# Attention scores in two parts: the low part of q against the high part of k as two 64-row matmuls in two halves of the array

## The reference

```
s = einsum('bqkgd,bskd->bkgqs', q, k) * HEAD_DIM ** -0.5      # 8 query heads, 2 key heads, HEAD_DIM = 64
p = softmax(s, axis=-1)                                       # over 256 context + 1024 latent keys
o = einsum('bkgqs,bskd->bqkgd', p, v)
```

## Time and profile before

| | |
|---|---|
| median of 3 runs | 2757.2 us (2756.16 to 2759.43) |
| profiled execution: its own time | 2757.11 us |
| its span in the trace | 2755.3 us |
| mean granted TensorE clock | 0.991 |
| TensorE busy (PE), weight loads (PEld) | 97%, 80% of the span |
| VectorE, ScalarE, GpSimd busy | 58%, 31%, 37% |
| scores (L900) on the chain that ended last | 6% |

### The profile page before, as it was taken

The page is one execution under the profiler, slowest core; times in us unless marked ns, Lnnn a source line. Parts: engine busy times, 40 slices in busy tenths (PEclk is TensorE's granted clock), DMA queues, the critical chain, the costliest instruction groups (busy, mean ns, idle before and its releaser), DMA issues.

```text
span 2755.3 us, 32885 instructions
## 1 busy us (share of the span) xinstructions
PE 2672.7 (97%) x13578; PEld 2196.3 (80%) x13578; DVE 1585.6 (58%) x1512; ACT 841.1 (31%) x1220; POOL 1021.2 (37%) x915
## 2 busy tenths in 40 slices
PE   7999999999999999999999899999999999999996
PEld 4888888888887888888878688888888888877874
DVE  3745544541018888847657763555552299866756
ACT  3234444442100000034314423545552000005313
POOL 3721111112224333334575662111114355554573
PEclk9999999999999999999999999999999999999998
DMA  6111111111255111124333512101112211114433
GB/s 264 35 60 35 39 35 39 35 41 62 76 188 212 44 38 39 39 90 149 133 128 126 173 41 69 43 35 35 39 43 81 77 46 47 46 58 145 142 124 113
DMA packets 75892, 224.74 MB, mean 82 GB/s; under 512 B 8672, under 2 KB 12000, under 8 KB 74720
## 3 DMA queue, kind: packets, MB, share of 16 engines
q1 hardware_dynamic: 53280, 182.26, 19.3%
q10 hardware_dynamic: 22464, 40.38, 3.9%
HBM read 177.52 MB, written 45.09 MB: 81 GB/s over the span
## 4 chain that ended last, share of the span: by engine, by line
PE 88%; DVE 6%; ACT 3%; issue 2%; DMA 1%; POOL 0%; SPq 0%; ACTq 0%; DVEq 0%; POOLq 0%
PE PS L733 48%; PE PS L864 20%; PE PS L900 6%; PE PS L922 5%; PE PS L909 5%; PE PS L932 1%; ACT Pr L1205 1%; DVE cv L1683 1%; PE PS L776 1%; DVE e L1756 1%; DMA wmA<-wmod 1%; ACT PTh L1228 1%; PE PS L782 1%; PE PS L886 0%; DMA wraw<-w 0%
## 5 line engine op out<-in xcount | busy, mean ns | idle before, releaser
L622 POOL CAST wh<-wraw 128x512 fp32r<-128x512 f32 (+1 forms) x424 | 333.7, 787 | 1262.8 <-PE PS L733 630.6
L624 POOL TENSOR_TENSOR wl<-wraw,wh 128x512 fp32r<-128x512 f32 (+1 forms) x424 | 611.2, 1441 | 34.0
L1650 DVE TENSOR_TENSOR PTl<-PS,PTh 128x512 fp32r<-128x512 f32 x328 | 226.9, 692 | 417.6 <-ACT PTh L1228 417.5
L733 PE MATMUL PS<-Uh,wh 128*128 128x512 f32 (+1 forms) x1536 | 428.8, 377 | 15.3 <-issue 9.6
L1683 DVE SCALAR_TENSOR_TENSOR cv<-hc,vec,cv 128x1024 f32<-128x1024 f32 x360 | 435.8, 1238 | 8.8
L733 PE MATMUL PS<-Uh,wl 128*128 128x512 f32 (+1 forms) x1536 | 420.4, 371 | 0.0
L733 PE MATMUL PS<-Ul,wh 128*128 128x512 f32 (+1 forms) x1536 | 418.7, 370 | 0.0
L864 PE MATMUL PS<-Uh,wh 128*128 128x512 f32 (+1 forms) x960 | 358.7, 374 | 2.8 <-POOL wl L624 2.3
L864 PE MATMUL PS<-Uh,wl 128*128 128x512 f32 (+1 forms) x960 | 357.1, 372 | 0.0
L864 PE MATMUL PS<-Ul,wh 128*128 128x512 f32 (+1 forms) x960 | 356.9, 372 | 0.0
L1228 ACT ACTIVATE PTh<-PS 128x512 fp32r<-128x512 f32 x328 | 196.2, 598 | 438.8 <-PE PS L909 434.2
(11 more groups left out here) (159 smaller groups left out, 3446.3 us busy)
## 6 DMA issues: line engine op xcount, KB each, us to landing
wraw<-w SPq DMA_DIRECT2D x164, 512.0 KB, 3.4
graw<-stg ACTq DMA_DIRECT2D x88, 256.0 KB, 2.0
wmB<-wmod SPq DMA_DIRECT2D x32, 512.0 KB, 5.7
e<-graw SPq DMA_DIRECT2D x24, 640.0 KB, 3.9
wraw<-w SPq DMA_DIRECT2D x48, 256.0 KB, 4.1
e<-graw SPq DMA_DIRECT2D x24, 512.0 KB, 3.6
wmA<-wmod SPq DMA_DIRECT2D x8, 1024.0 KB, 12.3
hL<-hT_in SPq DMA_DIRECT2D x8, 640.0 KB, 21.1
```

The lines of the kernel that those rows point to most:

```text
L622: nc.gpsimd.tensor_copy(wh[par][:, s], wraw[par][:, s]).then_inc(whi[par], 1)
L624: nc.gpsimd.tensor_tensor(wl[par][:, s], wraw[par][:, s], wh[par][:, s].bitcast(F32), ALU.subtract).then_inc(wsplit[par], 1)
L733: ins = mmul(PS[:, at + c:at + c + m], w[par][:, k * P:(k + 1) * P], x[:, k, c0 + c:c0 + c + m], start=(first and a == 0), stop=(last and ...
L1650: tt(PTl[b][:], PS[:, PT0[bank]:PT0[bank] + 512], PTh[b][:].bitcast(F32), ALU.subtract).then_inc(pt_free[bank], 1)
```

## The change

For a latent unit the three chunks are first multiplied with the high part of q. The low part of q is multiplied with the last chunk (keys 1024 to 1279) as before, with all 128 rows. For keys 0 to 511 and 512 to 1023 it is multiplied with 64 rows only: rows 0 to 63 of the stationary and the moving operand for the first, rows 64 to 127 for the second, into two PSUM banks. So that rows 64 to 127 hold the high part of k there, `k_lo` writes the low part of keys 512 to 1023 to rows 0 to 63. The product low by low, which the matmuls with all rows gave along, is left out for keys 0 to 1023. Context units do what they did.

```diff
@@ scores(un, h)
+                    hi, lo = (x[un % 2][:, h * P:(h + 1) * P] for x in (qTh, qTl))
                     for c, m in chunks(nk * P):
-                        for a, x in enumerate((qTh, qTl)):
-                            ins = mmul(PS[:, s0 + c:s0 + c + m], x[un % 2][:, h * P:(h + 1) * P],
-                                       kT[:, g, k0 * P + c:k0 * P + c + m], start=(a == 0), stop=(a == 1))
+                        mmul(PS[:, s0 + c:s0 + c + m], hi, kT[:, g, k0 * P + c:k0 * P + c + m], start=True, stop=False)
+                    ins = mmul(PS[:, s0 + c:s0 + c + m], lo, kT[:, g, k0 * P + c:k0 * P + c + m], start=False, stop=True)
+                    if nk > 2:
+                        for a in range(2):
+                            rows = slice(a * HD, (a + 1) * HD)
+                            ins = mmul(PS[:, s0 + a * 512:s0 + (a + 1) * 512], lo[rows], kT[rows, g, a * 512:(a + 1) * 512],
+                                       start=False, stop=True)
                     ins.then_inc(s_s, 1)
@@ k_lo(g)
                         dve.wait_ge(s_khi, 6 * l + 3 * g + i + 1)
-                        tt(kT[HD:P, g, c:c + n], tbank(f, n)[HD:P], kT[HD:P, g, c:c + n].bitcast(F32),
+                        rows = slice(0, HD) if i == 1 else slice(HD, P)
+                        tt(kT[rows, g, c:c + n], tbank(f, n)[rows], kT[rows, g, c:c + n].bitcast(F32),
                            ALU.subtract).then_inc(t_free[f % 2], 1)
```

## The result

The changed kernel took 2774.06 us (median of 5 runs, 2771.3 to 2774.68) against 2757.26 of the kernel before: 16.8 us slower (quotient of the medians 1.0061), ratio over all runs 1.0057 with a 95% interval of 1.0042 to 1.0071. A second series (5 runs against 15 of the kernel before) gave 1.0076 (1.0062 to 1.0089), 20.8 us. Forecast was + 20.

A forecast was written before the change was run, and what follows sets the result against it. TensorE was taken to set the pace, busy 97% of the span. Per head + 0.41 - 0.23 = + 0.18 us, times 128 + 23, less 3 absorbed: 2757 + 20 = 2777 us, range 2728 to 2797.

The forecast's parts named there:

- Counts and order: Attention scores: 128 score sums, each keeping six matmuls and six weight loads; the new order costs nothing.
- What is saved: 0.23 us a head: Low-part score matmuls: two halves side by side take one matmul's 0.23 us, saving at most 29 us over 128 sums.
- In 0.19, out 0.22, 0.41 together: TensorE around each 64-row pair: entering costs 0.19 us and leaving 0.22, together 0.41 us per head.
- The choice of 0 for the second half's load: Pair's weight loads: the second half's load adds 0 us; 0.11 more if it waits for the first.
- the one number taken over from another shape: Price of a trip into tiles and back, 0.33 us, read at L797's column tiles and applied to row halves.
- The 0.43 us that the prediction calls a full float32 matmul: At L782, 512 columns take 0.43 us start to start; L797's four tiles take the same, hence fully side by side.
- the loss before absorption: Each head's scores: 0.41 us trip less 0.23 saved gives + 0.18 us, times 128 + 23 us.
- The type costs nothing, the tiles' shape does: Around L782, full-width float32 between fp32r groups adds no time, so L797's 0.33 us comes from its tiles.
- What is absorbed: 3 us: Layer 1 attention: the exit is free at 15 heads whose next scores wait for the exponential, 15 x 0.22 = 3 us.
- Rival 1: Score pairs: row halves need no mode change, loads go ahead, 0.23 us a sum saved: 2728 us; chance 0.22.
- rival 2: Score pairs: entry 0.1 and exit 0.13 us cancel the saving, say one load hidden: 2757 within 5; chance 0.13.
- rival 3: Score pairs: halves don't run side by side and the mode changes too, 52 us less 3: 2806 us; chance 0.07.

The follow-up runs named there:

- order_swap: Changed kernel with the 64-row matmuls replaced by full 128-row ones, keeping the new order and k's swapped halves: 2753.1 us against 2754.05 before, ratio 1.0000.
- same_half: Changed kernel with both 64-row matmuls on the same rows and k's halves not swapped, so they cannot overlap: 2805.48 us against 2754.05 before, ratio 1.0188.
- pair_twice: Changed kernel with the two 64-row matmuls made twice, alternating first and second half: 2808.86 us against 2756.43 before, ratio 1.0192.
- two_trips: Changed kernel with the low 256-column matmul on 128 rows placed between the two 64-row matmuls: 2854.12 us against 2756.43 before, ratio 1.0362.
- pair_first: Changed kernel with the two 64-row matmuls ahead of the three high matmuls, behind the transposes: 2769.11 us against 2756.43 before, ratio 1.005.
- odd_heads: Changed kernel with the 64-row matmuls first, only at each unit's second and fourth head; other heads use all rows: 2756.87 us against 2754.7 before, ratio 1.0011.

## Why the prediction was right, step by step

*Counts and order.* Right: the order alone made no difference (order_swap).

*What is saved: 0.23 us a head.* Right, though taken from column tiles: the pair without overlap costs just that more (same_half), a second pair that overlaps costs just that too (pair_twice).

*In 0.19, out 0.22, 0.41 together.* Measured 0.40, with the open loads at the 0.11 us of the earlier trace rows. In: load at 1971.37 instead of 1971.28, 0.09, and the load itself open, 0.11. Out: from the pair's load to the next record it is 0.43 us, of which 0.11 is that load and 0.23 the stream, so 0.09 is left; and that next record stands 0.34 us before the one behind it instead of 0.23, 0.11 for its own open load. Together 0.20 in and 0.20 out. The stretch came out at 0.98 us, forecast 0.99, and a steady unit of layer 1 grew by 0.65, forecast 0.5 to 0.7. The choice of 0 for the second half's load was right: both load records stand in one row of 0.19 us. That the price of 32-column tiles in float32 holds for row halves in fp32r was the one number taken over from another shape; it held within 0.01 us. (The 0.43 us that the prediction calls a full float32 matmul is one of its two records; L797's groups are counted in records too, so the sum stands.) Behind this the loss before absorption is 0.17 us a head, forecast 0.18.

*The type costs nothing, the tiles' shape does.* The reading of the earlier trace rows against the earlier trace rows decided the sign of the forecast. The runs bear it out: here everything around the pair is fp32r, the type never changes, and the trip costs 0.40 us all the same, and 0.39 for a second one (two_trips).

*What is absorbed: 3 us.* This step was wrong in its mechanism. It said that the way out, behind the last matmul of the sum, is free at the 15 heads of layer 1 where the next scores wait. The interval from key tile 0 to key tile 2 nevertheless grew from 5.35 to 5.51 us, and the waits of layer 1 shrank from 4.5 to 4.2 us in all, not by 3. The timelines of ScalarE and VectorE in the changed kernel show why:

```profile
1973.47 0.60 ACT L1236 ACTIVATE PTh<-PS 128x512 fp32r<-128x512 f32 x1 [1.61 <-PE PS L917]
1973.96 0.59 ACT L1218 ACTIVATE ob<-PS 128x512 f32<-128x512 f32 x1
1974.44 1.33 ACT L1213 ACTIVATE Pr<-PS,nm 128x1280 f32<-128x1280 f32 x1
...
1972.09 1.48 DVE L1631 TENSOR_REDUCE nm<-PS 128x1 f32<-128x1280 f32 x1
```

The exponential stands on ScalarE behind two copies, and the first waits for the transposes of TensorE's next step, which come after the way out. VectorE's row maximum had started at 1972.09 and lasted 1.48 us: it was there 0.87 us before the exponential began. The chain of a wait led back over TensorE. The rows of the kernel before showed this already: in the earlier trace rows the maximum is over at 1930.43 and the exponential begins at 1931.13, 0.70 us later, behind

```profile
1930.16 0.60 ACT L1228 ACTIVATE PTh<-PS 128x512 fp32r<-128x512 f32 x1 [1.93 <-PE PS L909]
1930.65 0.59 ACT L1210 ACTIVATE ob<-PS 128x512 f32<-128x512 f32 x1
```

The prediction added up maximum and exponential without asking what else lay between them. What can be hidden in this wait is the way in, if the pair stands first (pair_first, odd_heads). All in all the attention grew by 20.0 us where 127 x 0.17 = 21.6 was the gross. What became of the missing 1.6 us is open: the interval up to the fourth head, for one, grew by 0.14 us instead of 0.17, which I have not traced further. That the 3 us taken off for a wrong reason brought the forecast to just the + 20 that the attention shows is luck; without them it would have been + 23.

*The rivals.* Rival 1 (no change of mode for row halves) falls with the open load records; rival 2 (the two sides cancel, say since one of the two loads is hidden) falls with them too, as both loads are open, and 16.8 us lie outside its 5; rival 3 (no overlap) was built as same_half, and cost 51.4 us, forecast 52 - 3. The rule in the Trainium skill, TensorEngine Tiling (Array Packing), section Key Properties, that changing the mode drains TensorE and changing the tile doesn't, agrees with this case on both counts: 0.39 us for a second trip, and 0.23 us, a plain stream, for a second pair. The Trainium skill, TensorE: Matmul & The Clock Gate, Part 3: Packing small matmuls, says that a load is pulled ahead of running matmuls when its row group doesn't conflict with theirs, or when it goes to the background weight buffer. A load for half the rows behind a matmul on all of them is not the first case, and by the second it would have gone ahead too, if it had such a target, which no run here can show. It did not: in the changed kernel all 128 loads of a first half start 0.20 to 0.21 us after the 256-column matmul, which has streamed after 0.12. From one half to the other the trace agrees with it: the two loads stand in one row of 0.19 us, where two on the same rows take 0.29 (same_half).

## What to carry to other kernels

Half the array's rows for a small product save one stream, 0.23 us for 512 columns here, but in these traces each switch between full and half rows lets the stream before it run out first and lays the next weight load open, 0.40 us for there and back. By these numbers it would pay only beyond 0.40 / 0.23, or 1.7, saved streams of 512 columns per trip, an estimate that no run here tested; one head's low part saves one. A tiled matmul already in the trace, here a column-tiled one in another stage, gave the price of the trip in advance; and before a wait is counted as cover, follow it back to see whether it doesn't lead over the very engine whose delay it is to hide.

## What the runs showed of the hardware

- Two 64-row matmuls of 512 columns in fp32r on different rows overlap wholly (changed kernel); their two 128-column loads stand in one row of 0.19 us. On the same rows the second adds 0.23 us (same_half).
- A trip from 128 rows to 64 and back cost 0.40 us in fp32r, close to what a trip to 32-column tiles cost in float32, 0.33 us with its narrower load. I had not expected the price to carry over so well between shapes.
- A way in that stands behind a wait, where TensorE has been idle for 0.28 us, costs nothing more: the interval before that head stays at 5.34 us (pair_first).
